# Seven block products in place of eight for the gate and value tiles of a convolutional feed-forward layer

## What is computed

```python
def conv_ffn(h, w_up, conv_w, conv_b, w_down):
    u = h @ w_up                                   # 1024 -> 2 * 2816
    u = conv(u, conv_w, width 3, causal, per channel) + conv_b
    gate, val = split(u, 2)
    return (silu(gate) * val) @ w_down             # 2816 -> 1024
```

## Time and profile before

| what | value |
|---|---|
| median of 3 runs | 2773.89 us |
| profiled execution, its own time | 2778.58 us |
| its span | 2776.6 us |
| granted TensorE clock, mean | 0.970 |
| TensorE / VectorE / GpSimd / ScalarE busy | 93% / 51% / 32% / 28% |
| first feed-forward, first matmul to last sum of squares | 554.3 to 1300.5 us |
| second feed-forward | 2003.1 to 2745.4 us |

### The profile page before, as it was taken

How to read it: one execution, slowest core, us unless ns; L and a number is a source line. 1 busy time by engine, 2 the same in 40 slices (tenths; PEclk the granted TensorE clock), 3 DMA queues, 4 the chain that set the end, 5 groups by cost and what they waited for, 6 DMA issues and landing times.

```text
span 2776.6 us, 32261 instructions
## 1 busy us (share of the span) xinstructions
PE 2576.6 (93%) x12444; PEld 2072.7 (75%) x12444; DVE 1407.1 (51%) x1641; ACT 782.4 (28%) x1337; POOL 881.6 (32%) x619
## 2 busy tenths in 40 slices
PE   7899999899999999997799999979799999999994
PEld 4688888578888888884577787757488888888883
DVE  4476674653333333336767677653743333333337
ACT  3344441221111111113346565551321111111111
POOL 4222112453333333333531323112553333333332
PEclk9999999999999999998999999979899999999997
DMA  3121133011111111111211312032011111111111
GB/s 130 49 76 64 62 113 130 30 38 46 46 54 46 45 53 45 45 53 48 91 50 43 92 46 76 24 144 98 23 44 48 46 49 50 45 48 51 45 45 61
DMA packets 44436, 166.19 MB, mean 60 GB/s; under 512 B 5552, under 2 KB 6064, under 8 KB 40880
## 3 DMA queue, kind: packets, MB, share of 16 engines
q1 hardware_dynamic: 36592, 132.14, 14.9%
q10 hardware_dynamic: 7744, 32.66, 3.0%
HBM read 129.65 MB, written 20.97 MB: 54 GB/s over the span
## 4 chain that ended last, share of the span: by engine, by line
PE 79%; DVE 12%; ACT 4%; DMA 1%; issue 1%; SPq 1%; POOL 1%; ACTq 0%; POOLq 0%; DVEq 0%
PE ps L893 11%; PE ps L894 11%; PE ps L895 11%; PE ps L914 6%; PE ps L915 5%; PE ps L916 5%; PE ps L789 3%; PE ps L687 3%; PE ps L689 3%; PE ps L688 3%; PE ps L761 2%; DVE a L1290 2%; PE ps L763 2%; PE ps L762 2%; PE ps L826 2%; PE ps L806 2%
## 5 line engine op out<-in xcount | busy, mean ns | idle before, releaser
L893 PE MATMUL ps<-h,w_hi 128*128 128x512 f32 x1408 | 551.0, 391 | 8.5 <-POOL h L567 7.7
L894 PE MATMUL ps<-h,w_hi 128*128 128x512 f32 x1408 | 549.2, 390 | 0.0
L895 PE MATMUL ps<-h,w_lo 128*128 128x512 f32 x1408 | 549.2, 390 | 0.0
L1503 DVE SCALAR_TENSOR_TENSOR tg<-ps,cv,tg 128x1023 f32<-128x1023 f32 x88 | 112.9, 1283 | 799.4 <-ACT tg L1205 799.4
L548 POOL TENSOR_TENSOR w_lo<-w_raw,w_hi 128x1024 fp32r<-128x1024 f32 x194 | 469.0, 2418 | 15.6
L546 POOL CAST w_hi<-w_raw 128x1024 fp32r<-128x1024 f32 x194 | 204.9, 1056 | 790.4 <-PE ps L763 275.8
L1205 ACT ACTIVATE tg<-ps,cv 128x1024 f32<-128x1024 f32 x88 | 106.3, 1208 | 994.2 <-PE ps L895 994.2
L545 POOL TENSOR_TENSOR gate<-ones 128x1 f32<-128x1 f32 x120 | 23.4, 195 | 945.7 <-PE ps L895 520.2
L893 PEld LDWEIGHTS ps<-h,w_hi 128*128 128x128 f32 x1408 | 265.2, 188 | 70.0 <-POOL h L567 13.2
L895 PEld LDWEIGHTS ps<-h,w_lo 128*128 128x128 f32 x1408 | 265.2, 188 | 55.3
L894 PEld LDWEIGHTS ps<-h,w_hi 128*128 128x128 f32 x1408 | 265.3, 188 | 54.5
(11 more groups left out here) (176 smaller groups left out, 4435.4 us busy)
## 6 DMA issues: line engine op xcount, KB each, us to landing
w_raw<-in_W SPq DMA_DIRECT2D x194, 512.0 KB, 3.3
h<-o_dram ACTq DMA_DIRECT2D x2, 6144.0 KB, 21.1
dsw<-draw SPq DMA_DIRECT2D x64, 128.0 KB, 2.3
o_dram<-most SPq DMA_DIRECT2D x6, 1024.0 KB, 4.2
o_dram<-dost SPq DMA_DIRECT2D x6, 1024.0 KB, 4.6
x<-in_x ACTq DMA_DIRECT2D x8, 512.0 KB, 9.8
x<-in_x ACTq DMA_DIRECT2D x1, 4096.0 KB, 12.9
x_dram<-x ACTq DMA_DIRECT2D x2, 2048.0 KB, 7.2
```

What stands on the lines that cost most here:

```text
L893: pe.matmul(out, wh, xh, start=k == 0, stop=False)
L894: pe.matmul(out, wh, xl, start=False, stop=False)
L895: last = pe.matmul(out, wl, xh, start=False, stop=k == KT - 1)
```

## The change

The gate and value tiles of a unit are seen as a product of 2 x 2 blocks: rows gate and value weights, columns the two halves of the tokens, and the width of 1024 split into two halves of 512 (G1, G2, V1, V2 the weight blocks, B11, B12, B21, B22 the token blocks). The Winograd form of Strassen's scheme makes the four results from seven block products, P1 to P7, each 4 steps of three matmuls.

- GpSimd forms S1 = V1 + V2, S2 = S1 - G1, S3 = G1 - V1, S4 = G2 - S2 of each unit's weights, and casts and splits nine half-size items (G1, S2, G2, S1, S3, V2, S4, and the two halves d1 and d2 of the down weights) into a ring of five slots.
- The token sums T1 = B12 - B11, T2 = B22 - T1, T3 = B22 - B12, T4 = B21 - T2 are made once per layer, by VectorE and GpSimd, and rounded by ScalarE; VectorE makes 20 of the 28 remainders, GpSimd 8. Some of them take the room of x, so x is written to DRAM (by ScalarE's queue) and read back (by SP's) in the last unit.
- The products rotate through PSUM banks 0 to 3. ScalarE copies P1; VectorE makes the seven results U2, C11, W, C22, U3, C21, C12 in SBUF, each from SBUF and one PSUM bank. The convolution then reads SBUF.
- The down product is made for one unit at a time: 6 matmuls per output f, 8 outputs and 8 adds per unit, placed after P7, P4 and P3 of the next unit.
- All loops over units are written out. The accumulator isn't cleared: the first unit's adds are copies.

```diff
+PRODUCTS = ["P1", "P6", "P2", "P5", "P7", "P4", "P3"]
+FIRST_PRODUCTS = ["P1", "P2", "P5", "P6", "P7", "P4", "P3"]
+WEIGHT_OF = {"P1": "G1", "P2": "G2", "P6": "S2", "P7": "S3", "P5": "S1", "P4": "V2", "P3": "S4"}
+TOKENS_OF = {"P1": "B11", "P2": "B21", "P6": "T2", "P7": "T3", "P5": "T1", "P4": "T4", "P3": "B22"}
+RING_SLOT = {"G1": 0, "S2": 1, "G2": 2, "S1": 3, "S3": 4, "d1": 0, "V2": 1, "S4": 2, "d2": 3}
+FIRST_ITEMS = ["G1", "G2", "S1", "S2", "S3", "V2", "S4"]
+ITEMS = ["G1", "S2", "G2", "S1", "S3", "d1", "V2", "S4", "d2"]
+RESULTS = ["U2", "C11", "W", "C22", "U3", "C21", "C12"]
+RESULT_OF = {"P6": "U2", "P2": "C11", "P5": "W", "P7": "U3", "P4": "C21", "P3": "C12"}
+LAST_ITEMS = ["d1", "d2"]
+N_ITEMS = len(FIRST_ITEMS) + (HT - 1) * len(ITEMS) + len(LAST_ITEMS)
+CASTS = [(c, k) for c in ("B11", "B21", "T1", "T2", "T3", "T4", "B22") for k in range(KH)]
+TAILS_DVE = [(c, k) for c in ("B11", "B21", "T1", "T2", "T3") for k in range(KH)]
+TAILS_POOL = [(c, k) for c in ("T4", "B22") for k in range(KH)]
+SCALED = list(range(KT)) + [KT + k + 4 * e for k in range(KH) for e in range(2)]
...
+        ring = [at(f"ring{r}", s_, 1, F32R) for r, s_ in enumerate((2, 3, 4, 5, 49))]
+        raw_d = at("raw_d", 48, 1)
+        s1 = at("s1", 50, 1)
+        x_r = at("x_r", 30, 8, F32R)
+        t2_r = at("t2_r", 38, 4, F32R)
+        cx = at("cx", 42, 4)
+        hid = at("hid", 42, 4, F32R)
+        cy = at("cy", 46, 2)
...
+                def item(n, name, free):
+                    at_ = ring[RING_SLOT[name]]
+                    count = item_count(layer, n, name)
+                    pool.wait_ge(free[0], free[1])
+                    pool.tensor_copy(half_of(at_, 0, 0), raw[name]).then_inc(item_hi, 1)
+                    pool.wait_ge(item_hi, count)
+                    pool.tensor_tensor(half_of(at_, 0, 1), raw[name], half_of(at_, 0, 0).bitcast(F32), ALU.subtract
+                                       ).then_inc(item_ready, 1)
...
+                    loaded("V", n)
+                    pool.tensor_tensor(raw["S1"], half_of(w_raw, 1, 0), raw["V2"], ALU.add).then_inc(w_sum, 1)
+                    pool.wait_ge(w_sum, count + 1)
+                    pool.tensor_tensor(raw["S3"], raw["G1"], half_of(w_raw, 1, 0), ALU.subtract).then_inc(w_sum, 1)
+                    pool.wait_ge(w_sum, count + 2)
+                    pool.tensor_tensor(raw["S2"], raw["S1"], raw["G1"], ALU.subtract).then_inc(w_sum, 1)
...
+                loaded("G", 0)
+                item(0, "G1", before[0])
+                item(0, "G2", before[0])
+                norm_help(2 * layer + 1, tails=False)
+                sums(0)
+                item(0, "S1", before[1])
+                item(0, "S2", before[1])
+                item(0, "S3", before[1])
+                for k in range(KH):
+                    pool.wait_ge(b_t1, KH * layer + k + 1)
+                    b12, b22 = half_of(a, k, 1), half_of(a, KH + k, 1)
+                    pool.tensor_tensor(b12, b22, b12, ALU.subtract).then_inc(b_t3, 1)
+                for k in range(KH):
+                    pool.wait_ge(b_t2, KH * layer + k + 1)
+                    pool.wait_ge(b_lo_dve, len(TAILS_DVE) * layer + TAILS_DVE.index(("B21", k)) + 1)
+                    b21 = half_of(a, KH + k, 0)
+                    pool.tensor_tensor(b21, b21, half_of(cy, k // 2, k % 2), ALU.subtract).then_inc(b_t4, 1)
+                item(0, "V2", up_of(0, "P6"))
+                for k in range(KH):
+                    tail("T4", k)
+                last_sum(0)
+                item(0, "S4", up_of(0, "P2"))
+                for k in range(KH):
+                    tail("B22", k)
+                for n in range(1, HT):
+                    loaded("G", n)
+                    item(n, "G1", up_of(0, "P1") if n == 1 else down_of(n - 2, 3))
+                    sums(n)
+                    item(n, "S2", up_of(n - 1, "P4"))
+                    item(n, "G2", up_of(n - 1, "P3"))
+                    item(n, "S1", up_of(0, "P5") if n == 1 else down_of(n - 2, 7))
+                    item(n, "S3", up_of(n - 1, "P7"))
+                    loaded("D", n - 1)
+                    item(n, "d1", up_of(n, "P1"))
+                    item(n, "V2", up_of(n, "P6"))
+                    last_sum(n)
+                    item(n, "S4", up_of(n, "P2"))
+                    item(n, "d2", up_of(n, "P5"))
+                loaded("D", HT - 1)
+                item(HT, "d1", down_of(HT - 2, 3))
+                item(HT, "d2", down_of(HT - 2, 7))
...
+                def down(n, f):
+                    part = f // 4
+                    at_ = ring[RING_SLOT[("d1", "d2")[part]]]
+                    if f % 4 == 0:
+                        pe.wait_ge(item_ready, item_count(layer, n + 1, ("d1", "d2")[part]))
+                        pe.wait_ge(hid_lo, u0 + n + 1)
+                    if n > 0 or f >= 2:
+                        pe.wait_ge(acc_done, down_count(layer, n, f) - 2)
+                    f4 = f % 4
+                    wh, wl = at_[:, 0, f4 * P:(f4 + 1) * P], at_[:, 0, HB + f4 * P:HB + (f4 + 1) * P]
+                    for half in range(2):
+                        out = bank(4 + 2 * (f % 2) + half)
+                        xh, xl = half_of(hid, 2 * (n % 2), half), half_of(hid, 2 * (n % 2) + 1, half)
+                        pe.matmul(out, wh, xh, start=True, stop=False)
+                        pe.matmul(out, wh, xl, start=False, stop=False)
+                        last = pe.matmul(out, wl, xh, start=False, stop=True)
+                    last.then_inc(dn_done, 1)
+                for n in range(HT):
+                    for place, product in enumerate(PRODUCTS if n else FIRST_PRODUCTS):
+                        up(n, place, product)
+                        if n and product in ("P7", "P4"):
+                            down(n - 1, ("P7", "P4").index(product))
+                    if n:
+                        for f in range(2, KT):
+                            down(n - 1, f)
+                for f in range(KT):
+                    down(HT - 1, f)
...
+                    g0, g1, v0, v1 = g[:, 0:HB], g[:, HB:T], v[:, 0:HB], v[:, HB:T]
+                    dst, src, product, needs = {
+                        "U2": (v0, g0, "P6", None), "C11": (g0, g0, "P2", None), "W": (g1, v0, "P5", "U2"),
+                        "C22": (v1, g1, "P7", "W"), "U3": (v0, v0, "P7", "U2"), "C21": (v0, v0, "P4", "U3"),
+                        "C12": (g1, g1, "P3", "W")}[name]
+                    dve.wait_ge(up_done, up_count(layer, n, product))
+                    if name == "U2":
+                        dve.wait_ge(bank_copied, u0 + n + 1)
+                    if needs:
+                        dve.wait_ge(c_sum, result_count(layer, n, needs))
+                    dve.tensor_tensor(dst, src, up_bank(n, product), ALU.add).then_inc(c_sum, 1)
...
+                for n in range(HT):
+                    result(n, "U2")
+                    if n:
+                        product(n - 1)
+                    result(n, "C11")
+                    if n:
+                        hid_tail(n - 1)
+                    for name in ("W", "C22", "U3"):
+                        result(n, name)
+                    if n:
+                        add(n - 1, 0)
+                    result(n, "C21")
+                    if n:
+                        add(n - 1, 1)
+                    conv_tile(n, 1)
+                    result(n, "C12")
+                    if n:
+                        for f in range(2, KT):
+                            add(n - 1, f)
+                    conv_tile(n, 0)
+                product(HT - 1)
+                hid_tail(HT - 1)
...
+                for i in range(KT):
+                    scaled(i)
+                    if i >= 1:
+                        tail(*TAILS_DVE[i - 1])
+                dve.wait_ge(x_rstd, 2 * n + 2)
+                for k in range(KH):
+                    scaled(KT + k)
+                    scaled(KT + KH + k)
+                    if k == 0:
+                        tail(*TAILS_DVE[KT - 1])
+                    b11, b12, b22 = half_of(a, k, 0), half_of(a, k, 1), half_of(a, KH + k, 1)
+                    dve.wait_ge(b_lo_dve, len(TAILS_DVE) * layer + TAILS_DVE.index(("B11", k)) + 1)
+                    dve.wait_ge(b_f, 2 * KT * layer + SCALED.index(KT + KH + k) + 1)
+                    dve.tensor_tensor(b11, b12, b11, ALU.subtract).then_inc(b_t1, 1)
+                    dve.wait_ge(b_t1, KH * layer + k + 1)
+                    dve.tensor_tensor(half_of(cy, k // 2, k % 2), b22, b11, ALU.subtract).then_inc(b_t2, 1)
+                    if k >= 1:
+                        tail("T1", k - 1)
+                tail("T1", KH - 1)
+                for c in ("T2", "T3"):
+                    for k in range(KH):
+                        tail(c, k)
...
-                        for half in range(2):
-                            out = bank(4 + 2 * (f % 2) + half)
-                            for k in range(2):
```

(42 more changed lines are left out.)

365 lines of the change are left out of this document (205 added, 160 removed).

## The result

The changed kernel takes 2819.33 us in the median (2816.74 to 2820.14, 4 runs); the kernel before, in the same session, 2775.20 (2773.20 to 2776.72, 4 runs). The ratio is 1.0158, 95% interval 1.0140 to 1.0175: slower by 44 us, where 20 us slower was forecast (2794). The time lies inside the range, and the sign is right, but the change of time is more than twice the forecast. The profiled execution has a span of 2817.4 us against 2776.6.

A forecast was written before the change was run, and what follows sets the result against it. TensorE's matmul count and waits bound the middle, VectorE and GpSimd chains both ends. Layer 1 +11.0 and layer 2 +9.5 make +20.5 us, 2794 us as a median; range 2735 to 2848.

The forecast's parts named there:

- The matmuls removed: In each feed-forward layer, 12 matmuls of each of 22 units go from TensorE: 59.8 us less per layer.
- The start: Start of a layer: VectorE and GpSimd chains leave TensorE idle 47.5 us before unit 1's P6, +39.8 us per layer.
- wrong if P6 starts before 610: Test at the start of a layer: the prediction is wrong if unit 1's P6 starts before 610 us.
- taps of 2.2 us and more: Sign of collision: the convolution's taps take 2.2 us and more next to GpSimd's operations, 1.28 elsewhere.
- The end: End of a layer: the last unit's chain and outputs at VectorE's pace add 18.2 us in layer 1, 16.7 in layer 2.
- The middle: Loop over units in a layer: waits on adds and on a collision at G2 add 12.8 us per layer.
- The cycle is 29.92 + 0.6 + 0.3 = 30.8: Time per unit in the loop: 132 matmuls 29.92 us, waits on adds 0.6, collision at G2 0.3, together 30.8.
- the 0.6 us of the adds: In each unit, TensorE's waits on VectorE's adds ahead of outputs 4 and 6: 0.6 us.
- the 0.3: In each unit, P2's wait for G2, whose cast and remainder collide with the gate tile's taps: 0.3 us.
- the ring: Loop of waits, not priced as such: output 3 frees G1's slot, GpSimd works through G2, P2 waits for it.
- rival (4): Collision takes over the loop, pushing G2, S1 and S3 past their products: 1.2 us per unit, 2844 us, chance 0.20.
- wrong if the cycle is under 30.3: Test in the loop: the prediction is wrong if the time per unit is under 30.3 us, its break-even.

The follow-up runs named there:

- e5: Changed kernel with P5 computed twice in every unit but the first, 12 matmuls more per unit: 2934.3 us, ratio 1.0583 to the kernel before.
- d2: Changed kernel with the gate tile's two taps cut to 2 and 1 columns in all units but the last: 2783.6 us, ratio 1.0044 to the kernel before.
- d1: Changed kernel with the value tile's two taps cut to 2 and 1 columns in all units but the last: 2811.8 us, ratio 1.0155 to the kernel before.

## Why the prediction was right in sign and too small in size

**The matmuls removed: right, as far as shown.** -59.8 us per layer; e5 measured the price of 12 more as 2.69, against 2.72 a product.

**The start: right.** Forecast were 47.5 us of idle TensorE before P6 of unit 1; 67.8 us with 96 matmuls (21.8) leave 46.0. Another 1.7 us went where the prediction had 2 in its range: after 4.69 us without a matmul the clock granted from 616.3 to 620.0 is 0.50, the 1.2 GHz level, the matmuls are 0.43 apart, and unit 1 needs 30.4 us from its P6 to the next P1 (30.8 in the second layer), where 28.7 is the rule. The way there was much as drawn, once both are counted from the layer's first matmul (554.3 in the forecast, 548.5 now): VectorE finished its remainders after 41.8 us (42.7 forecast), and GpSimd's chain from V2's cast to S2's remainder took 27.6 (29.5). Timelines of GpSimd and TensorE after:

```profile
591.46 4.99 POOL L745 TENSOR_TENSOR x_r<-a,x_r 128x512 fp32r<-128x512 f32 x4
...
599.67 6.98 POOL L745 TENSOR_TENSOR h<-a,h 128x512 fp32r<-128x512 f32 x4
...
611.25 2.12 POOL L735 TENSOR_TENSOR w_raw<-s,w_raw 128x512 f32<-128x512 f32 x1
613.43 1.48 POOL L714 CAST ring<-w_raw 128x512 fp32r<-128x512 f32 x1
615.00 1.27 POOL L716 TENSOR_TENSOR ring<-w_raw,ring 128x512 fp32r<-128x512 f32 x1
...
616.32 0.80 PE L1062 MATMUL ps<-t_r,ring 128*128 128x512 f32 x1 [4.69 <-POOL ring L716]
```

T4's four remainders alone take 4.99, B22's beside the value tile's taps 6.98. My test "wrong if P6 starts before 610" passes with 616.3, and GpSimd has no gap from 588.7 on. The sign "taps of 2.2 us and more" next to GpSimd's operations holds at the start (2.16, 2.10) and not in the loop (1.89, 1.51).

**The end: right.** From the last matmul of unit 20's outputs to the stage's last sum 44.0 and 38.8 us were forecast; 42.9 and 40.5 came. Timelines after, answering to the earlier trace rows:

```profile
1275.04 0.40 PE L1082 MATMUL ps<-hid,ring 128*128 128x512 f32 x1
1285.14 0.76 PE L1080 MATMUL ps<-hid,ring 128*128 128x512 f32 x1 [9.71 <-DVE hid L1752]
...
1288.08 1.22 DVE L1762 TENSOR_TENSOR a<-a,ps 128x1024 f32<-128x1024 f32 x1 [1.96 <-PE ps L1082]
1290.42 1.23 DVE L1792 TENSOR_TENSOR ss<-ss,sq 128x1024 f32<-128x1024 f32 x1 [1.12 <-ACT sq L1408]
1291.57 1.21 DVE L1762 TENSOR_TENSOR a<-a,ps 128x1024 f32<-128x1024 f32 x1
```

10.1 us of chain between the units (10.7 forecast; 9.6 for 9.1 in the second layer), then 3.48 a step (3.49).

**The middle: this step failed.** "The cycle is 29.92 + 0.6 + 0.3 = 30.8" is wrong in its form and in one of its terms. The form: the 0.6 us of the adds arises after output 3, where GpSimd already works on G1; it runs beside the chain that ends in the 0.3. The cycle is the larger of two, TensorE's own 29.92 + 0.75 = 30.67 (d2) and the ring's 31.43, and d1 shows that a change of the smaller one changes nothing. The form alone did not make the forecast too low: with the forecast's own numbers the larger of the two is 29.92 + 0.6 = 30.5, further off still. The sum added 0.3 where it should not have and so hid a part of the error in the term. The term: by the forecast's own numbers the ring was 18.80 from P2 to output 3, 0.46 to G1 and 11.2 to the end of G2, 30.5 in all. Measured are 19.09, 0.53, 11.81 and 0.05 to P2 in the unit shown, 31.48. Of the 1.0 missing, 0.61 is GpSimd's chain: items of 1.94 and 1.92 for 1.86, sums of 1.37 for 1.33, and 3.83 for the item G2 where 3.45 was left for it. I had written "one of GpSimd's holds up VectorE by about 1.05" and its reverse, but had charged G2's two operations for one encounter and a fraction, when each of them met one of the two taps: 1.00 on the cast and 0.86 on the remainder. 0.29 is TensorE's stretch: the successor of the wait at 0.34 (+0.11), and the next 17 matmuls at 0.234 in the mean, 935.87 to 939.84 (+0.12), account for most of it; 0.07 is the start of G1 and 0.05 the way from G2 to P2. There is a slip in the term as well: it has P2's weights wanted at 5.2 of the unit, where the prediction's own walk starts P2 at 5.44, as in the trace without the wait (961.03 to 966.47). With a G2 that ends at 5.4 it had no wait at all to charge.

The Trainium skill, "SBUF — State Buffer", Who interferes with whom, says that an instruction of VectorE with two SBUF inputs and one of GpSimd that reads SBUF exclude each other, and that one with a single SBUF input does not contend. The runs agree on both, which the earlier trace rows could not show for 1024 columns: the first tap went from 1.28 to 1.89 here, while the results, each from SBUF and a PSUM bank, stay at 0.69 and the adds at 1.22 beside GpSimd's work.

In numbers: (31.43 - 30.8) x 42 = 26.5 us more, so 20.5 + 26.5 = 47.0 for the two stages, and +47.3 was measured; start and end were each off by 1 to 2 us and cancelled, which is luck. The median, 2819, lies midway between the forecast's 2794 and rival (4)'s 2844. In its mechanism (4) was the nearest of the rivals: it named the collision as what takes over the loop, but it put its victim at S1 and S3, and G2 alone did it. By the test "wrong if the cycle is under 30.3" the forecast stood; it had no such test for a cycle that is too long, and that was the side on which it was exposed.
